# PEER value sum: from 512-column token-major products plus transposes to eight 128-column feature-major products per slot

## The reference, cut to what matters

```
ub = u[eb]; vb = v[eb]
act = gelu(einsum('cd,ced->ce', xb, ub), approximate=False) * gb
y   = einsum('ce,ced->cd', act, vb)
x   = x + y
```

## Time and profile before

| | |
|---|---|
| runs | 1826.63, 1819.50, 1819.37 us; median 1819.5 us |
| profiled execution | span 1819.3 us; the page gives no other time of its own for it |
| instructions | 24081 |
| PE / PEld busy | 1606.3 us (88%) / 1203.9 us (66%) |
| DVE / ACT / POOL busy | 1209.1 us (66%) / 835.9 us (46%) / 362.2 us (20%) |
| slot gathers | 268.45 MB of 421.15 MB moved |
| slot products (1024 matmul records) | 493.2 us busy |

### The profile page before, as it was taken

One profiled execution on the slowest core, in us unless ns is written; L12 is line 12 of the kernel. 1 busy time (PEld: TensorE's weight loads), 2 busy tenths in 40 slices (PEclk: granted clock), 3 DMA queues, 4 the chain that ended last, 5 costly groups with the idle time before them and its releaser, 6 DMA issues.

```text
span 1819.3 us, 24081 instructions
## 1 busy us (share of the span) xinstructions
PE 1606.3 (88%) x9325; PEld 1203.9 (66%) x9325; DVE 1209.1 (66%) x2403; ACT 835.9 (46%) x1701; POOL 362.2 (20%) x327
## 2 busy tenths in 40 slices
PE   7878998689887778878888988879999999999999
PEld 6768998555432223222243778869999875579999
DVE  5677556788788888454655767556765547567764
ACT  5555544445444444333534632335554335345542
POOL 1010012335354445434441003000000100010000
PEclk9889999899999999999999989999999999899999
DMA  6322452799999999999996311224445431035544
GB/s 258 126 83 93 159 189 93 314 388 424 426 423 427 427 426 427 427 427 427 427 426 280 116 70 47 81 82 162 164 163 167 157 110 52 1 107 184 185 164 151
DMA packets 63593, 421.15 MB, mean 231 GB/s; under 512 B 8180, under 2 KB 11512, under 8 KB 15608
## 3 DMA queue, kind: packets, MB, share of 16 engines
q0 software_dynamic: 36864, 268.45, 35.1%
q1 hardware_dynamic: 23952, 148.70, 22.7%
q10 hardware_dynamic: 2664, 2.47, 0.4%
HBM read 418.54 MB, written 1.05 MB: 231 GB/s over the span
## 4 chain that ended last, share of the span: by engine, by line
PE 61%; DMA 17%; DVE 13%; ACT 7%; issue 2%; POOL 0%; SPq 0%; ACTq 0%; DVEq 0%; POOLq 0%
PE bank L306 59%; DMA uv<-in_uv,idx 15%; DVE lows L369 3%; DVE uv L1363 2%; ACT dg L318 2%; PE bank L2533 1%; ACT L318 1%; DMA slabs<-in_w_in 1%; ACT acts L318 1%; PE bank L311 1%; DVE cacc L322 1%; ACT wp L314 1%; ACT wf L314 1%; DVE t L322 0%; POOL uv L1477 0%
## 5 line engine op out<-in xcount | busy, mean ns | idle before, releaser
L306 PE MATMUL bank<-uv,dg 128*128 128x512 f32 x1024 | 493.2, 617 | 105.1 <-ACT dg L318 102.8
L306 PEld LDWEIGHTS bank<-uv,dg 128*128 128x128 f32 x1024 | 181.2, 191 | 406.0 <-ACT dg L318 247.9
L1363 DVE CUSTOM_DVE_ANT_0 uv<-uv,htok 128x1024 f32<-128x1024 f32 x256 | 313.0, 1223 | 170.3 <-DMA uv<-in_uv,idx 168.3
L1477 POOL DMA_INDIRECT uv<-in_uv,idx x256 | 283.0, 1106 | 379.2 <-PE bank L306 331.5
L369 DVE TENSOR_TENSOR lows<-slabs,wp 128x2048 fp32r<-128x2048 f32 (+1 forms) x78 | 167.7, 2150 | 50.3 <-ACT wp L314 49.9
L306 PE MATMUL bank<-hn,lows 128*128 128x272 f32 (+2 forms) x704 | 200.9, 285 | 0.0
L484 POOL TENSOR_TENSOR sqT<-sqT 128x256 f32<-128x256 f32 (+1 forms) x42 | 46.3, 1103 | 685.5 <-ACT sqT L318 683.2
L318 ACT ACTIVATE acts<-acts 128x1 f32<-128x1 f32 x256 | 51.3, 200 | 281.7 <-DVE acts L1363 281.3
L314 ACT ACTIVATE wp<-slabs 128x2048 fp32r<-128x2048 f32 (+1 forms) x78 | 140.5, 1802 | 81.6 <-DMA slabs<-in_dn 28.5
L306 PE MATMUL bank<-hh,lows 128*128 128x272 f32 x448 | 134.5, 300 | 0.0
L306 PEld LDWEIGHTS bank<-hn,lows 128*128 128x128 f32 x704 | 132.6, 188 | 0.0
(11 more groups left out here) (383 smaller groups left out, 3020.7 us busy)
## 6 DMA issues: line engine op xcount, KB each, us to landing
slabs<-in_up SPq DMA_DIRECT2D x44, 1024.0 KB, 4.8
slabs<-in_w_in SPq DMA_DIRECT2D x28, 1024.0 KB, 4.9
slabs<-in_dn SPq DMA_DIRECT2D x32, 704.0 KB, 4.0
slabs<-in_wkv SPq DMA_DIRECT2D x8, 1024.0 KB, 6.0
slabs<-in_w_out SPq DMA_DIRECT2D x8, 1024.0 KB, 4.8
slabs<-in_pq SPq DMA_DIRECT2D x8, 1024.0 KB, 5.2
slabs<-in_wq SPq DMA_DIRECT2D x4, 1024.0 KB, 4.8
slabs<-in_wo SPq DMA_DIRECT2D x4, 1024.0 KB, 4.8
```

Of the source, the lines that this page charges most:

```text
L306: ins = T.e.matmul(pr[2] if len(pr) > 2 else out, pr[0], pr[1], start=(start and k == 0), stop=(stop and k == len(pairs) - 1), skip_group_ ...
L1363: V.e.tensor_tensor_reduce(u_, u_, htok[:, n, :], 1.0, 0.0, ALU.mult, ALU.add, acts[:, n, e_:e_ + 1]).then_inc(*V.up("dot", q))
L1477: G.e.indirect_dma_start(uv[q % NU][:, :], None, d["uv"][:, :], bass.IndirectOffsetOnAxis(ap=idx[:, n, e_:e_ + 1], axis=0)).then_inc(s_uv[ ...
```

## The change

Per slot, TensorE takes the v rows as stationary operand, 128 features at a time, and dg as moving operand of 128 columns: eight products instead of two. Each gives 128 features on the partitions by 128 tokens, and lies in its quarter of the same banks as before; the first product of a bank at slot 0 starts the bank. The per-slot semaphore counts stay at two, after the fourth and the eighth product. The sum is then feature-major already; VectorE adds the banks to XR straight from PSUM. The copies to ytok, the transposes and their waits are gone, and so is ScalarE's wait for the transposes in fin_scalar. The scratch view is renamed.

```diff
@@ -229,7 +229,7 @@
             pij = sbuf(ph, "pij", [P, 2, 16], U32)
             sm = sbuf(ph, "sm", [P, 2])
         zero.close()
-        ytok = sqT[:, :, :].rearrange("p c t -> p (c t)")
+        sqf = sqT[:, :, :].rearrange("p c t -> p (c t)")
         HH = [sbuf(top, f"hh{q}", [P, NC, T2], F32R) for q in range(2)]
         whl = sbuf(top, "whl", [P, 2, SLOTW], F32R)
         with ExitStack() as ph:
@@ -1205,8 +1205,8 @@
 
 
         EARLY = 2 * P - 50
-        SQE = ytok[:, 0:8 * 144].rearrange("p (c t) -> p c t", c=NC)
-        SQL = ytok[:, 1088:1088 + D].rearrange("p (c t) -> p c t", c=NC)
+        SQE = sqf[:, 0:8 * 144].rearrange("p (c t) -> p c t", c=NC)
+        SQL = sqf[:, 1088:1088 + D].rearrange("p (c t) -> p c t", c=NC)
 
         def gf2(c):
             return sub[:, c, :]
@@ -1369,14 +1369,9 @@
         def added_vector(n):
 
             for half in range(2):
-                hs = slice(half * 512, half * 512 + 512)
                 V.wait_ge(*T.at("y", n * P + P - 1, half))
-                V.wait_ge(*(T.at("early") if n else T.at("htok", 1, 1)))
-                V.e.tensor_copy(ytok[:, hs], B[4 + 2 * n + half][:, :]).then_inc(*V.up("ytok", n, half))
-            for half in range(2):
-                V.wait_ge(*T.at("yT", n, half))
                 xs = XR[:, 4 * half:4 * half + 4, n * P:n * P + P]
-                V.e.tensor_tensor(xs, B[half][:, :].rearrange("p (c t) -> p c t", c=4), xs, ALU.add).then_inc(*V.up("peer_x", n, half))
+                V.e.tensor_tensor(xs, B[4 + 2 * n + half][:, :].rearrange("p (c t) -> p c t", c=4), xs, ALU.add).then_inc(*V.up("peer_x", n, half))
 
         def early_vector(k):
             at = VCOL["an0"][0]
@@ -1521,19 +1516,11 @@
                     T.wait_ge(*A.at("htok", 1, 1))
                     T.wait_ge(s_uv[q % NU], 16 * (q // NU + 1))
                     for half in range(2):
-                        mm(B[4 + 2 * n + half][:, :], [(dg[q % NDG][:, :], uv[q % NU][:, D + half * 512:D + half * 512 + 512])],
-                           e_ == 0, e_ == P - 1).then_inc(*T.up("y", q, half))
-                    if e_ == P - 1:
-                        for half in range(2):
-                            T.wait_ge(*V.at("ytok", n, half))
-                            if n:
-                                T.wait_ge(*V.at("peer_x", 0, half))
-                            else:
-                                T.wait_ge(*V.at("ev", "pq", 7, half))
-                            for r in range(4):
-                                c = 4 * half + r
-                                ins = tr(B[half][:, r * P:r * P + P], ytok[:, c * P:c * P + P], P)
-                            ins.then_inc(*T.up("yT", n, half))
+                        for r in range(4):
+                            c = 4 * half + r
+                            ins = mm(B[4 + 2 * n + half][:, r * P:r * P + P], [(uv[q % NU][:, D + c * P:D + c * P + P], dg[q % NDG][:, :])],
+                                     e_ == 0 and r == 0, e_ == P - 1)
+                        ins.then_inc(*T.up("y", q, half))
 
 
 
@@ -1556,8 +1543,6 @@
                 A.wait_ge(*V.at("peer_x", 1, half))
                 for c in range(4 * half, 4 * half + 4):
                     act(HH[0][:, c, 144:T2], XR[:, c, P:T1], ACT.Copy, scale=gfa[:, c:c + 1]).then_inc(*A.up("an0", "hi", c))
-                if half == 0:
-                    A.wait_ge(*T.at("yT", 1, 1))
                 act(SQL[:, 4 * half:4 * half + 4, :], XR[:, 4 * half:4 * half + 4, P:T1], ACT.Square).then_inc(*A.up("an0", "sq", half))
             stage_wait(A, "peer")
             split_scalar(N_L2 + 2)
```

## The result

| | runs | median us (lowest to highest) | ratio to before, 95% interval |
|---|---|---|---|
| before | 20 | 1821.8 (1817.2 to 1830.3) | |
| changed | 20 | 1828.2 (1821.8 to 1833.5) | 1.0026 [1.0013, 1.0038] |
| changed again, on another chip (12 runs beside 35 of before) | 12 | 1826.9 | 1.0017 [1.0001, 1.0033] |

The forecast was 1.0 us faster, 1818.5, with 1814 to 1825. The medians of the two sets of 20 lie 6.4 us apart and their means 4.7; I use the ratio. By it the change costs 4.7 us (0.0026 x 1821.8; interval 2.4 to 6.9), and 3.1 us in the repeat: under the 0.5% that the chances call "same", but clear of noise, and slower. The level moved as well: three runs of before had a median of 1819.5, larger sets had 1821.8 to 1826.2.

The account below looks back on a forecast made before the run. The prediction took memory to bound the slot stage at about 427 GB/s, 2.45 us a slot, with TensorE nearly full afterwards. Its terms, -1.4 + 0.4 + 0 + 0 = -1.0 us, gave 1818.5 us, range 1814 to 1825.

Parts of the forecast that it names:

- same: Whole kernel: a measured time within about 0.5% (9.1 us) of before; chance 0.86.
- Where the 0.07 is not covered: Head of the slot stage: added 0.07 us per slot delays ids and first gathers; 0.4 us slower, bounds 0 to 0.8.
- one visible hole at 380 us: Head, 380 to 382 us: DMA engines nearly empty, share 0.04, as GpSimd waits for ids; to grow hardly wider.
- TensorE becomes the bound while the head projections run: Head projections, to about 520 us: at 0.141 us a record TensorE outlasts the memory; 1834 us, chance 0.07.
- The clock: Rival for the slot stage: TensorE falls to 1.2 GHz; 2050 us or more, chance 0.05 together with no overlap.
- The sum: Whole kernel: end -1.4, head +0.4, other terms 0, together -1.0 us.
- the one narrow group among slots: Sixteen narrow float32 records from 925.10 to 926.89 in the old trace, taken as the new slot's pace, 1.79 us.
- the narrow pace of 0.112 us a record: Slot products back to back: sixteen records take 1.79 us against 1.72 before, +0.07 us a slot.
- 2.05 us for a lone slot: Steady slots: a lone slot's products take 2.05 us against 1.98, inside 0.45 us of idle time, so no cost.
- starts 2.45 us apart: Steady slots: starts stay at the memory's pace, 1 MB gathered per slot at 427 GB/s, 2.45 us.
- the stall between the blocks: At slot 127: removing TensorE's 3.65 us wait gains nothing, at most 1 us; rival says 1815 us, chance 0.04.
- the end: After slot 255: direct additions bring the first w_in2 product forward by 1.4 us, bounds 1.0 to 1.7.

Follow-up runs that it names:

- E5: Kernel before plus two more float32 products of 128 columns in each of slots 0 to 47; 1.0075 [1.0052, 1.0099].
- E6: Kernel before plus two more float32 products of 128 columns in each of slots 136 to 183, in block 1; 0.9989 [0.9971, 1.0007].
- E16: Kernel before plus one narrow product in every third of slots 0 to 47, 0.07 us a slot; 1.0016 [0.9998, 1.0034].
- E10: Kernel before with the second product of slots 1 to 47 cut from 512 to 424 columns; 1.0016 [1.0003, 1.0029].
- E8: Block 0 wide, block 1 narrow, plus eight wide products of constants in the wait for the first gather; against the kernel before 0.9990 [0.9972, 1.0008].

## Why the prediction was wrong

**The term that failed** is the head of the stage, "Where the 0.07 is not covered": I took 0.4 us, with 0.8 as upper end. Between six profiles each, the slot stage grew by 660.6 - 657.8 = 2.8 us (standard errors 0.7 and 0.4), and all of it had come by the gather of slot 80, which starts 3.1 us later behind the first one (means of 212.4 and 209.3 us). The reasoning counted the slots ahead of one visible hole at 380 us and took DMA share 1.01 behind it as proof that nothing further was exposed. The share did say that the memory was busy, not how near to empty its queue was. E5 and E6 show the difference: dosed alike, the head loses and the steady part doesn't. The rival "TensorE becomes the bound while the head projections run" had the right place for the cost of pace, with a wrong point: I let it begin at 2.0 us a slot, computed from the mean spare time of 11.7 us per 100. At 1.79 the cycle above is 0.4 us longer already. My reading, which no run isolates, is that spare time in waits (the 1.6 us for dg behind each head's scores, VectorE's qp) is no room for work that comes at another moment.

**The clock** is the other half of the failed term. The sum put it at nothing, with the reason that the one narrow group among slots kept its clock; that group stands in the steady part, and says nothing of the head. As a rival I had it only for the whole stage, at 2050 us. It came in small: a dip in five of six narrow heads, 1.6 us of one cycle where it falls at 47 us. In the steady part dips come in the kernel before too, and the memory kept 427 GB/s through one (granted 0.96).

**Right:** the narrow pace of 0.112 us a record from one group of 16; 2.05 us for a lone slot; starts 2.45 us apart; nothing from the stall between the blocks; the end, 1.28 us against 1.4, step by step. The ratio of two and a half that the Trainium skill's figures for narrow and wide products give ("TensorE: Matmul & The Clock Gate", "Back-to-back issue gap") is not what these float32 products do: 518.1 against 493.2 us busy is 1.05.

**The sum as measured:** +2.8 - 1.3 = +1.5 us in the profiles. The timings say 4.7 (2.4 to 6.9) and 3.1 (0.2 to 6.0). The rest, 1.6 to 3.2 us by the middles, I can't place. The run's time goes with its mean granted clock: over all runs, with a level of its own for each kernel and set, 0.9 us per 0.001. The changed kernel's 20 runs have a mean clock of 0.9645, the kernel before 0.9650 to 0.9671 in four later sets. In the twelve profiles the time at 1.2 GHz within the slot stage is the same, 36 us in the mean with a wide head and 35 with a narrow one; over the whole span it is 127 (112 to 137) and 134 us (122 to 146). Whether the change lowers the clock outside the stage, or these are differences of chips and moments, stays open.

**The level and the range.** The median of three runs was 2.3 us below that of twenty. That put the whole range low, and its upper end at 1825 had room for one run's spread but not for it, the head and the rest together.

A version that takes the end's gain and leaves the head alone is E1: block 0 wide with its transposes hidden between the blocks, block 1 narrow. 0.9993 [0.9978, 1.0008]: its interval lies below the changed kernel's first one, overlaps the repeat's, and doesn't show it to beat the kernel before.

## What to carry to other kernels

That a resource is saturated on average doesn't say that it covers another engine everywhere; before you cost added work at nothing, look at the stretch where the other engine also has its own long pieces, and count all slots of that stretch, not those before the hole you can see. When a product is turned to save a transposition, do it in the block whose result is waited for, and leave it where the transposes are hidden. An effect of 0.1% needs the stage's own length from several profiles: the code up to the first gather, which no run touched, took from 328.3 to 338.7 us. And look at the clock in every profile before you read a small dose in it: a dip of 1.6 us is as large as the effect that E16 was to show.

## What the hardware showed that I had not expected

A kernel with less work in one stretch could be slower: E10 removed 7 us of TensorE work from the head and measured 1.0016 [1.0003, 1.0029], with two dips, at 44 and 71 us, that the fuller head didn't have. Where the clock was kept up at one place (E8, 1.00 where it was 0.50), dips stood at 43 and 71 us, where E1 has none. And the most heavily loaded head, E5's, had no dip at all.
